# A transformer pair on one core: decays and SiLU moved in two rounds of the Delta net, U before AT, shorter head norms in the stick, gates spread

## The chip, the cores and the metric

One Trainium2 chip, one NeuronCore. The metric is the device time of one execution in microseconds; it is the median of several runs. Nothing is shared with other cores, and all inputs lie in HBM at the start.

## The reference, cut to what matters

The function is a first block (modulated SwiGLU, an attention with short convolution, SwiGLU; 512 tokens and a context of 256) followed by a second block on 528 tokens (16 meta tokens ahead). All is float32. The change touches the second block's mixer:

```
proj = hn @ w_in                                   # 1024 -> 89 column tiles of 128
q = l2norm(silu(conv(dq))); k = l2norm(silu(conv(dk))); v = silu(conv(dv))
g = cumsum(-exp(a_log) * softplus(da + dt_bias))   # decays, per chunk
# Delta net, 8 heads, state 128 x 256, chunk by chunk:
decay = exp(where(i >= j, g_i - g_j, -inf))
lower = where(i > j, (k*beta) @ k.T * decay, 0);   U = inverse of (eye + lower)
attn = q @ k.T * decay                             # AT is its transpose
u, w = U @ (v*beta), U @ (k*beta*exp(g))
v_new = u - w @ S;  o = (q*exp(g)) @ S + attn @ v_new;  S = S*exp(g_last) + k_dec.T @ v_new
o_dn = rmsnorm(o) * silu(dz)
# stick breaking attention, 8 heads:
qs = rmsnorm(sq, sbq_gain);  ks = rmsnorm(sk, sbk_gain)
z = qs @ ks.T * 128**-0.5;  w = exp(log_sigmoid(z) + sum of later log_sigmoid(-z)), strictly causal
merged = sigmoid(gate_dn) * (o_dn @ w_branch_dn) + sigmoid(gate_sb) * (o_sb @ w_branch_sb)
h = h + merged @ w_out
```

## The kernel before

**Products.** Activations lie with features on the partitions. Each weight tile of 1024 x 128 is loaded by SyncE's queue into one of three `w_raw` buffers, copied by ScalarE into `w_hi` (fp32r) and the rest is computed into `w_lo` by VectorE or GpSimd (`lows`; the table `LOW`, line 394, says which, by number of the tile). Four pairs of hi and lo exist (`PARTS`). A product is `w_hi*x_hi + w_hi*x_lo + w_lo*x_hi`, eight row tiles k of it, each one `mm` event (`quantum`, line 1098). `highs(m)` and `lows(m)` work up to four tiles ahead of tile m, and wait for the product that used the buffer before.

**One order for all engines.** The second block's mixer is driven by two lists of events, `DELTA` and `STICK`, that Python makes before the kernel is emitted. `timed` and `merged` put small events between the `mm` and `branch` events, at times in us given by tables (`PREPARE`, `SCAN`, `L2NORM`, `LATE_SCAN` and so on). Every engine walks the same list in the same order and does its own part of each event; engines are in order, so an event that waits on one engine holds what stands behind it in the list. Semaphores (`p_u`, `k_norm`, ...) count finished steps.

**A round of the Delta net.** Round i runs the scan of head i (`v0`, `s0`, `k1`, ... `s4`, `nsq`, `norm`, `gain`, `parts`, `hiz`), prepares head i+1 (`pair`, `turn`, then six levels `x1`, `u1`, ... `u6` that invert the triangle), broadcasts and exponentiates the decays of head i+2 (`bcast`, a DMA from HBM on ScalarE's queue, and `decay`), normalises its q and k (`l2q`, `lnq`, `stq`), and multiplies the branch weights of head i-1 (`branch`). `decay` is done by ScalarE (five Relu, two Exp into `DT`, one Exp of `gB`; line 1967 on), VectorE (the mask on `DT`, two steps) and GpSimd (`LT`). The last chunk has 16 tokens only, so work on chunks comes in two blocks: four chunks of 128 and one of 16 (`WIDE`).

**pair and turn.** `pair` (tensor: line 1359) makes k k' and k q' for both blocks: the first block's products in one half bank each, both products of the small block in a third. VectorE (`pairs`, line 2696) makes from them, for the first block, `LT`, U in two steps and `AT`, then the same four steps for the small block; `p_u` counts these eight steps. `turn` (line 1368) transposes U of each block, ScalarE copies it out, GpSimd masks `LT` into `LM`, then come `x1` and its copies.

**Banks.** `Banks` hands out PSUM at build time. Small events of the Delta net use a ring of four half banks in turn; each entry remembers the semaphore value at which its bank is free. `pair` takes three entries, of which the second is given back at `p_u` 8h+4 (AT of the first block) and the third at 8h+8; `s0` takes two, `turn` two. Big products and branches have a ring of two double banks: a projection tile holds one, so that successive branch products use the other and wait for VectorE's add into `acc`. A tile's bank is free once ScalarE has copied it (`projected`); the copy of a z tile of head h waits until `parts` of head h-1 has used `ZZ`.

**Stick norms.** Squares (ScalarE), a product with ones (`nq`, `nk`), Ln and Exp on ScalarE for y = v^-1/2, then VectorE: v from PSUM, one Newton step in three instructions, and the gain; for q one more for the factor 128^-0.5. `k_v` frees the bank, `k_norm` counts three per head.

**Gates.** Sixteen tiles (73 to 88) are gates; ScalarE keeps the first four raw and takes the sigmoid of the others as they come; VectorE multiplies `acc` and `accs` (`gate`), in the last two rounds of the stick and behind them.

**Start of the second block.** After the last product of the second SwiGLU, ScalarE does root_ln and root_exp, then `highs`; VectorE does `root_v` and `root`, then `lows`, then writes the normed input whose first tile PE waits for.

## Time and profile before

| | us |
|---|---|
| median of 3 runs | 2865.19 (2865.05 to 2865.75) |
| the profiled execution, its own time | 2861.57 |
| its span, first to last instruction | 2859.3 |
| TensorE busy | 2790.1 (98%) |
| VectorE busy | 1489.2 (52%) |
| ScalarE busy | 1139.2 (40%) |
| GpSimd busy | 513.2 (18%) |
| mean granted TensorE clock | 0.993 |

The profile is of one execution. Busy times are sums of instruction durations without overlap; matmuls are pipelined, so a stall of less than half a us hardly shows as idle time. The chain that ended last is PE for 87% of the span. The first block and its two SwiGLU take 0 to 1343 us, the Delta net 1343 to 2081, the stick and gates 2081 to 2443, the output product and the last SwiGLU the rest.

### The profile page before, as it was taken

Reading aid. Unit: us, or ns where it says so; the run is one execution under the profiler, and the core shown is the slowest. Engines: PE = TensorE matmul, PEld = TensorE weight load, DVE = VectorE, ACT = ScalarE, POOL = GpSimd, SP = SyncE. Lnnn points to the kernel's source line nnn. Section 1 sums busy time; section 2 is a strip of 40 time slices with the busy share of each in tenths; the row PEclk is TensorE's granted clock in tenths of the full one; section 3 lists DMA queues with packets and bytes.
Section 4 is the critical chain, followed back from the end, with each engine's and each line's share of the span. In section 5 each row is a group of like instructions: output and inputs, shape, how many; then the busy total and the mean of one; then the engine's idle time right before and its main releaser. Section 6 shows DMA issues by size and latency. Waiting matters only on the chain.

```text
span 2859.3 us, 37052 instructions
## 1 busy us (share of the span) xinstructions
PE 2790.1 (98%) x14453; PEld 2233.2 (78%) x14453; DVE 1489.2 (52%) x2096; ACT 1139.2 (40%) x1697; POOL 513.2 (18%) x297
## 2 busy tenths in 40 slices
PE   8999999999999999999999999999999999999999
PEld 4888888866656688887898888887868877788887
DVE  6734534257546633335754656554267775653443
ACT  4221212224444432223655555554466663432221
POOL 0000000023111100002444444434422223100000
PEclk9999999999999999999999999999999999999999
DMA  6422313143102322222211211111211112232222
GB/s 234 151 78 83 120 63 111 53 139 120 37 30 88 127 93 92 96 92 100 80 53 45 67 56 64 53 53 38 74 60 60 60 60 93 95 103 93 91 97 81
DMA packets 69871, 241.77 MB, mean 85 GB/s; under 512 B 8218, under 2 KB 8346, under 8 KB 69314
## 3 DMA queue, kind: packets, MB, share of 16 engines
q1 hardware_dynamic: 62032, 221.28, 22.9%
q10 hardware_dynamic: 7666, 18.13, 1.9%
q8 instruction: 116, 1.90, 0.3%
q14 instruction: 57, 0.47, 0.1%
HBM read 232.74 MB, written 6.64 MB: 84 GB/s over the span
## 4 chain that ended last, share of the span: by engine, by line
PE 87%; DVE 5%; ACT 5%; DMA 1%; issue 1%; ACTq 0%; DVEq 0%; POOL 0%; SPq 0%; POOLq 0%
PE ps L1098 61%; PE ps L1484 3%; PE ps L1288 2%; PE ps L1381 2%; PE ps L1257 2%; PE ps L1585 2%; PE ps L1421 1%; PE ps L1275 1%; PE ps L1128 1%; PE ps L1309 1%; PE ps L1413 1%; ACT r L461 1%; DVE UT L468 1%; PE ps L1266 1%; ACT w_hi L461 1%
## 5 line engine op out<-in xcount | busy, mean ns | idle before, releaser
L1098 PE MATMUL ps<-Nh,w_hi 128*128 128x512 f32 (+1 forms) x1808 | 660.5, 365 | 9.5 <-DVE Nl L468 4.9
L1098 PE MATMUL ps<-Nl,w_hi 128*128 128x512 f32 (+1 forms) x1808 | 630.0, 348 | 0.0
L1098 PE MATMUL ps<-Nh,w_lo 128*128 128x512 f32 (+1 forms) x1808 | 628.0, 347 | 0.0
L461 ACT ACTIVATE w_hi<-w_raw 128x1024 fp32r<-128x1024 f32 (+1 forms) x352 | 368.7, 1047 | 637.4 <-PE ps L1098 521.8
L468 POOL TENSOR_TENSOR w_lo<-w_raw,w_hi 128x1024 fp32r<-128x1024 f32 x125 | 308.0, 2464 | 750.4 <-ACT w_hi L461 746.7
L468 DVE TENSOR_TENSOR w_lo<-w_raw,w_hi 128x1024 fp32r<-128x1024 f32 (+1 forms) x227 | 281.8, 1242 | 257.5 <-ACT w_hi L461 247.8
L1098 PEld LDWEIGHTS ps<-Nh,w_hi 128*128 128x128 f32 x1808 | 342.6, 190 | 80.2 <-issue 30.1
L1098 PEld LDWEIGHTS ps<-Nl,w_hi 128*128 128x128 f32 x1808 | 342.7, 190 | 50.6 <-issue 5.8
L1098 PEld LDWEIGHTS ps<-Nh,w_lo 128*128 128x128 f32 x1808 | 342.4, 189 | 44.1
L1098 PE MATMUL ps<-x1h,w_hi 128*128 128x512 f32 (+1 forms) x784 | 272.3, 347 | 1.9 <-DVE x1l L479 1.9
L1098 PE MATMUL ps<-x1l,w_hi 128*128 128x512 f32 (+1 forms) x784 | 266.6, 340 | 0.0
L1098 PE MATMUL ps<-x1h,w_lo 128*128 128x512 f32 (+1 forms) x784 | 264.8, 338 | 0.0
L1098 PEld LDWEIGHTS ps<-x1h,w_hi 128*128 128x128 f32 x784 | 147.0, 187 | 37.4 <-issue 16.1
L1098 PEld LDWEIGHTS ps<-x1h,w_lo 128*128 128x128 f32 x784 | 147.5, 188 | 18.4 <-DVE w_lo L468 0.2
L1098 PEld LDWEIGHTS ps<-x1l,w_hi 128*128 128x128 f32 x784 | 147.3, 188 | 18.0 <-issue 1.4
L468 POOL TENSOR_TENSOR f_t<-f_t,f_t 128x768 f32<-128x768 f32 (+1 forms) x14 | 25.0, 1786 | 658.9 <-ACT f_t L461 658.9
L1098 PE MATMUL ps<-h1h,w_hi 128*128 128x512 f32 x352 | 118.7, 337 | 0.0
L1098 PE MATMUL ps<-h1l,w_hi 128*128 128x512 f32 x352 | 118.7, 337 | 0.0
L1098 PE MATMUL ps<-h1h,w_lo 128*128 128x512 f32 x352 | 117.7, 334 | 0.0
L468 DVE TENSOR_TENSOR f_t<-f_t,ps 128x768 f32<-128x768 f32 (+1 forms) x44 | 36.1, 821 | 134.2 <-PE ps L1098 133.3
L461 ACT ACTIVATE f_t<-ps 128x768 f32<-128x768 f32 (+1 forms) x44 | 31.1, 708 | 178.7 <-PE ps L1098 178.3
L479 DVE SCALAR_TENSOR_TENSOR ada_acc<-w_raw,sc,ada_acc 128x512 f32<-128x512 f32 x112 | 84.2, 752 | 5.6
(353 smaller groups left out, 4725.0 us busy)
## 6 DMA issues: line engine op xcount, KB each, us to landing
w_raw<-in_w_in SPq DMA_DIRECT2D x132, 512.0 KB, 3.5
w_raw<-in_w_proj SPq DMA_DIRECT2D x89, 512.0 KB, 3.4
w_raw<-in_w_ada SPq DMA_DIRECT2D x52, 512.0 KB, 4.1
w_raw<-in_w_out SPq DMA_DIRECT2D x48, 448.0 KB, 3.2
w_raw<-in_w_out SPq DMA_DIRECT2D x24, 512.0 KB, 3.4
w_raw<-in_w_mix_in SPq DMA_DIRECT2D x19, 512.0 KB, 3.5
w_raw<-in_w_bdn SPq DMA_DIRECT2D x16, 512.0 KB, 3.4
w_raw<-in_w_mix_out SPq DMA_DIRECT2D x8, 512.0 KB, 3.5
```

The costliest lines, as they stand in the source:

```text
L461: self.then_inc(self.e.activation(out, in_, func, **kw), sem)
L468: self.then_inc(self.e.tensor_tensor(out, a, b, op), sem)
L479: self.then_inc(self.e.scalar_tensor_tensor(out=out, in0=a, scalar=s, in1=b, op0=op0, op1=op1), sem)
L1098: ins = e.matmul(out[:, 512 * j:512 * j + n], a[:, kk, :], x[:, kk, c0:c0 + n], start=k == 0 and p == 0, stop=k == nt - 1 and p == 2)
L1128: ins = e.matmul(bank[0:2, 0:512], t.sc[:, 2 * k:2 * k + 2], a[:, i, :], start=k == 0, stop=k == KT - 1)
L1257: ins = e.matmul(out[:, c0:c0 + nn], t.qT[r0:r0 + 64, h // 2, qb * P:(qb + 1) * P], t.kT[r0:r0 + 64, h // 4, c0:c0 + nn], start=True, stop ...
L1266: ins = e.transpose(out[:, c0:c0 + P], t.pr[n % 2][:, i * P:(i + 1) * P], cs("ident"))
L1275: ins = e.matmul(ps[:, 6, :], t.vp[:, i, 2 * (h // 4) + h % 2, :], t.PT[h % 2][:, i, :], start=h % 2 == 0 and i == 0, stop=h % 2 == 1 and ...
L1288: ins = e.matmul(out, a[:, k, :], x[:, k, 0:TX], start=k == 0 and p == 0, stop=k == KT - 1 and p == 2)
L1381: ins = e.matmul(bank[0:n, c * n:(c + 1) * n], t.LM[lv % 2][0:n, c0 + c, 0:n], UT[0:n, 1, c0 + c, 0:n], start=True, stop=True)
L1484: ins = e.matmul(out[:, 0:TX], a[:, 2 * (k % 4) + x, :], b[:, x, MS], start=x == 0 and p == 0, stop=x == 1 and p == 2)
L1585: ins = e.matmul(out[:, 0:TX], a[:, k, :], b[:, 0, MS], start=p == 0, stop=p == 2)
```

## The change

1. Two tables more, `FIRST_ROUND` and `LAST_ROUND`, place `bcast` and `decay` in round 0 (head 2) and in round 5 (head 7). In the list, `decay` of head 2 moves from behind unit 12, `stk2` and `parts` to between `u6` and unit 12; that of head 7 from behind `parts` and the last branch to between `stk1` and `u6`. `siluv` of round 0 goes behind `s0` of round 1. In round 6 `v0` and `s0` come ahead of `turn` and `siluv` behind it.
2. `pairs` makes LT and U of both blocks, then AT of both. `p_u` counts in the new order, so the waits for the second block's U become 8h+6 and 8h+4, and the second bank of `pair` is given back at 8h+7.
3. The stick's norms: ScalarE squares y after Exp; VectorE computes (bank + 128 eps) * y^2, then (that - 384) * y, then the product with a gain that was scaled once (`gain_sb`); no separate factor for q.
4. `gate`: 73 to 75 and 76 to 78 at two points become 73-74, 75, 76-77, 78-79 and 80-81 at five.
5. Tile 3 of `w_proj` has its low part on VectorE instead of GpSimd; at the start of the second block `highs` and `lows` stand ahead of the root's steps.

```diff
...
 DECAYS = ((66, "bcast"), (73, "decay"))
+FIRST_ROUND = ((58, "bcast"), (65, "decay"))
+LAST_ROUND = ((58, "bcast"), (64.5, "decay"))
 SCAN = ((0.52, "v0"), (5.18, "s0"), (8.86, "k1"), (11.5, "v1"), (14.15, "s1"), (18.33, "k2"),
...
 L2_FIRST = ((21.01, "siluz"), (22.55, "siluqk"), (25.3, "l2q"), (25.3, "lnq"), (27.1, "stq0"), (30.4, "stq1"),
-            (30.4, "stq2"), (37, "l2k"), (40, "lnk"), (45.3, "stk0"), (45.9, "stk1"), (45.9, "stk2"),
-            (59.1, "siluv"))
+            (30.4, "stq2"), (37, "l2k"), (40, "lnk"), (45.3, "stk0"), (45.9, "stk1"), (45.9, "stk2"))
 L2_LAST = ((18.91, "siluz"), (21.38, "siluqk"), (22.99, "l2q"), (22.99, "lnq"), (25.08, "stq0"), (25.13, "stq1"),
            (27.17, "stq2"), (30.21, "l2k"), (30.71, "lnk"), (30.71, "stk0"), (33.94, "stk1"), (38.5, "stk2"))
 
 LATE_PREPARE = ((1.35, "pair"), (6.9, "turn"), (9.6, "x1"), (11.2, "u1"), (17.7, "x2"), (22.2, "u2"),
                 (28.2, "x3"), (32.7, "u3"), (35.7, "x4"), (40.2, "u4"), (46.7, "x5"), (49.7, "u5"),
                 (56.9, "x6"), (60.5, "u6"))
-LATE_SCAN = ((7.95, "v0"), (7.95, "siluv"), (7.95, "s0"), (7.95, "k1"), (9.83, "v1"), (12.1, "s1"),
+LATE_SCAN = ((0.52, "v0"), (7.3, "siluv"), (5.2, "s0"), (7.95, "k1"), (9.83, "v1"), (12.1, "s1"),
              (16.67, "k2"), (19.21, "v2"), (23.63, "s2"), (27.41, "k3"), (28.59, "v3"), (31.72, "s3"),
...
         if i + 2 < NH:
-            steps += [(at, s, i + 2) for at, s in DECAYS]
+            steps += [(at, s, i + 2) for at, s in (FIRST_ROUND if i == 0 else LAST_ROUND if i + 3 == NH else DECAYS)]
+            steps += [(5.2, "siluv", 0)] if i == 1 else []
             after += [(at, s, i) for at, s in (L2_FIRST if i == 0 else L2NORM if i + 3 < NH else L2_LAST)]
...
 _POOLED = [(split_of("w_mix_in", 4), split_of("w_mix_out", 0)),
-           (split_of("w_proj", 3), split_of("w_o2", 0))]
+           (split_of("w_proj", 4), split_of("w_o2", 0))]
 LOW = ["pool" if any(a <= m < b for a, b in _POOLED) else "dve" for m in range(len(SPLITS))]
...
 
-        self.k_raw, self.k_sq, self.k_mm, self.k_ln, self.k_v, self.k_exp, self.k_norm = (
-            new("k_raw"), new("k_sq"), new("k_mm"), new("k_ln"), new("k_v"), new("k_exp"), new("k_norm"))
+        self.k_raw, self.k_sq, self.k_mm, self.k_v, self.k_exp, self.k_norm = (
+            new("k_raw"), new("k_sq"), new("k_mm"), new("k_v"), new("k_exp"), new("k_norm"))
         self.z_mm, self.z_abs, self.z_ln, self.z_sp, self.vt_mm, self.vt = (
...
         self.eps_sq = mem.put("eps_sq", [P, 1])
+        self.gain_sb = mem.put("gain_sb", [P, 2])
         low = mem.at
...
         elif name == "pair":
-            for i, v in enumerate((1, 4, 8)):
+            for i, v in enumerate((1, 7, 8)):
                 chain.use((name, h, i), s.p_u, 8 * h + v)
...
         for i, (c0, n, C) in enumerate(WIDE):
-            w.wait_ge(s.p_u, 8 * h + 4 * i + 3)
+            w.wait_ge(s.p_u, 8 * h + 3 * i + 3)
             bank = ps[:, bank_of(("turn", h, i)), :]
...
         n = SIZES[jb]
-        w.wait_ge(s.k_norm, 3 * h + 3)
+        w.wait_ge(s.k_norm, 2 * h + 2)
         bank = ps[:, bank_of((f"z{jb}", h)), :]
...
     e.dma_start(h_spill, XV).then_inc(s.h_out, 16)
+    highs(split_of("w_proj", 0) - 1, last)
     root_ln(5, D, f[1], COLSX, None, t.eps_sq[:])
     root_exp(f[3], f[1])
-    highs(split_of("w_proj", 0) - 1, last)
     z4 = [tv[0], tv[2], f[0], f[1]]
...
     def head_norm(h, i, ev):
-        w.wait_ge(s.k_norm, 3 * h + 2 * i)
+        w.wait_ge(s.k_norm, 2 * h + i)
         for j, (c0, n) in enumerate(COLS2 if i else COLSM):
             w.wait_ge(s.k_mm, 3 * h + i + j + 1)
-            w.act(t.sr[0][:, c0:c0 + n], ps[:, B.of[(*ev, j)][0], 0:n], ACT.Ln, s.k_ln, scale=1.0 / P,
+            w.act(t.sr[0][:, c0:c0 + n], ps[:, B.of[(*ev, j)][0], 0:n], ACT.Ln, s.act_step, scale=1.0 / P,
                   bias=cs("eps", n=1))
         cc = slice(0, T2) if i else MS
-        w.act(t.sr[1][:, cc], t.sr[0][:, cc], ACT.Exp, s.k_exp, scale=-0.5)
+        w.act(t.sr[1][:, cc], t.sr[0][:, cc], ACT.Exp, s.act_step, scale=-0.5)
+        w.act(t.sr[0][:, cc], t.sr[1][:, cc], ACT.Square, s.k_exp)
 
...
     ffn(1, XV, t.h2h[:, :, 0:TX], t.h2l[:, :, 0:TX], f[0:2], f[2:4], COLSX, GX, t.GM[:, 1], last)
+    lows(split_of("w_proj", 0) - 1, last)
     root_v(5, D, f[0], COLSX, None, EPS * EPS)
     root(5, f[0], f[2], f[3])
-    lows(split_of("w_proj", 0) - 1, last)
     w.wait_ge(*summed(6, s, 6))
...
     def pairs(h):
+
+        def product(i, j, n, C):
+            bank = ps[:, B.of["pair", h, j][0], :] if i == 0 else ps[:, B.of["pair", h, 2][0], j * n:]
+            return in_chunks(bank, n, C)
+
         for i, (c0, n, C) in enumerate(WIDE):
-            b, b2 = (in_chunks(ps[:, B.of["pair", h, j][0], :] if i == 0 else ps[:, B.of["pair", h, 2][0], j * n:], n, C)
-                     for j in range(2))
-            dt, at, lt = (a[0:n, c0:c0 + C, 0:n] for a in (t.DT, t.AT[h % 2], t.LT))
+            lt = t.LT[0:n, c0:c0 + C, 0:n]
             u = t.UT[h % 2][0:n, 0, c0:c0 + C, 0:n]
             w.wait_ge(s.p_lt, 2 * h + i + 1)
             w.wait_ge(s.p_pair, 4 * h + 3 * i + 1)
-            w.tt(lt, lt, b, ALU.mult, s.p_u)
+            w.tt(lt, lt, product(i, 0, n, C), ALU.mult, s.p_u)
             w.tt(u, lt, each(cs("level", n, n, 0), n, C), ALU.mult, s.p_u)
             w.tt(u, each(cs("ident", n, n), n, C), u, ALU.subtract, s.p_u)
+        for i, (c0, n, C) in enumerate(WIDE):
+            at, dt = (a[0:n, c0:c0 + C, 0:n] for a in (t.AT[h % 2], t.DT))
             w.wait_ge(s.p_pair, 4 * h + 2 * i + 2)
-            w.tt(at, b2, dt, ALU.mult, s.p_u)
+            w.tt(at, product(i, 1, n, C), dt, ALU.mult, s.p_u)
 
...
 
+    for i, (name, factor) in enumerate((("sbq", -1.0 / 256 * float(P) ** -0.5), ("sbk", -1.0 / 256))):
+        w.ts(t.gain_sb[:, i:i + 1], sm(name), factor, None, ALU.mult, None, s.step)
+
     def head_norm(h, i, ev):
         cc = slice(0, T2) if i else MS
-        v, tt, y = t.sr[5], t.sr[0][:, cc], t.sr[1][:, cc]
+        tt, square, y = t.sr[5], t.sr[0], t.sr[1][:, cc]
+        w.wait_ge(s.k_exp, 2 * h + i + 1)
         for j, (c0, n) in enumerate(COLS2 if i else COLSM):
-            w.wait_ge(s.k_ln, 3 * h + i + j + 1)
-            w.ts(v[:, c0:c0 + n], ps[:, B.of[(*ev, j)][0], 0:n], 1.0 / P, EPS, ALU.mult, ALU.add, s.k_v)
-        w.wait_ge(s.k_exp, 2 * h + i + 1)
-        w.stt(tt, y, -0.5, v[:, cc], ALU.mult, ALU.mult, s.step)
-        w.tt(tt, tt, y, ALU.mult, s.step)
-        w.stt(y, tt, 1.5, y, ALU.add, ALU.mult, s.step)
+            w.stt(tt[:, c0:c0 + n], ps[:, B.of[(*ev, j)][0], 0:n], P * EPS, square[:, c0:c0 + n], ALU.add, ALU.mult, s.k_v)
+        w.stt(y, tt[:, cc], -384.0, y, ALU.add, ALU.mult, s.step)
         dst = t.Fs[h % 2][:, i, cc]
-        w.stt(dst, dst, sm("sbq" if i == 0 else "sbk"), y, ALU.mult, ALU.mult, s.k_norm)
-        if i == 0:
-            w.ts(dst, dst, float(P) ** -0.5, None, ALU.mult, None, s.k_norm)
+        w.stt(dst, dst, t.gain_sb[:, i:i + 1], y, ALU.mult, ALU.mult, s.k_norm)
 
...
             if gating is not None and ev[0] == "mm" and ev[3] == 1:
-                for u in {77: (73, 74, 75), 78: (76, 77, 78)}.get(gating, (gating,)):
+                for u in {77: (73, 74), 78: (75,), 79: (76, 77), 80: (78, 79), 81: (80, 81)}.get(gating, (gating,)):
                     gate(u)
...
         for i, (c0, n, C) in enumerate(WIDE[:XC[lv] - XC[lv - 1]]):
-            w.wait_ge(s.p_u, 8 * h + 4 * i + 1)
+            w.wait_ge(s.p_u, 8 * h + 3 * i + 1)
             if lv > 2:
...
```

## Rows read from the trace of the kernel before

**Rows 1.** Page, parts 1 and 5.
```profile
PE 2790.1 (98%) x14453; PEld 2233.2 (78%) x14453; DVE 1489.2 (52%) x2096; ACT 1139.2 (40%) x1697; POOL 513.2 (18%) x297
...
L468 DVE TENSOR_TENSOR w_lo<-w_raw,w_hi 128x1024 fp32r<-128x1024 f32 (+1 forms) x227 | 281.8, 1242 | 257.5 <-ACT w_hi L461 247.8
```

**Rows 2.** Waits of PE, 1343 to 2450 us: us in total, times, longest.
```profile
PE ps L1368 <- DVE UT L468: 7.6, 4, 3.5
PE ps L1368 <- DVE AT L468: 6.0, 6, 1.2
PE ps L1449 <- ACT V L461: 5.4, 3, 4.4
...
PE ps L1553 <- DVE SP L468: 4.2, 1, 4.2
PE ps L1471 <- ACT r L461: 3.1, 2, 2.1
```

**Rows 3.** Stretches: us, busy of PE, PEld, DVE, ACT, POOL, clock, DMA, GB/s.
```profile
1375.60:1379.10 3.50, 3.50 (x15) 3.20 (x14) 3.32 (x4) 3.35 (x5) 1.24 (x1) 0.51 0.09 29
1942.30:1952.50 10.20, 7.74 (x26) 6.01 (x27) 4.06 (x7) 4.32 (x8) 4.32 (x5) 0.50 0.15 53
1611.20:1618.00 6.80, 5.54 (x41) 4.89 (x39) 3.95 (x9) 2.01 (x5) 5.62 (x5) 1.00 0.47 155
```

**Rows 4.** Timeline of PE, turns of heads 1, 3: start, us, instructions, idle before.
```profile
1453.15 0.63 PE L1368 MATMUL ps<-const,UT 128*128 128x128 f32 x4 [0.99 <-DVE AT L468]
1454.04 0.17 PE L1368 MATMUL ps<-const,UT 16*16 16x16 f32 x1 [0.25 <-DVE AT L468]
...
1613.18 0.60 PE L1368 MATMUL ps<-const,UT 128*128 128x128 f32 x4
```

**Rows 5.** Timeline of VectorE, pairs of head 3.
```profile
1612.29 0.69 DVE L468 TENSOR_TENSOR AT<-ps,DT 128x512 f32<-128x512 f32 x1
...
1613.50 0.92 DVE L468 TENSOR_TENSOR UT<-LT,const 16x16 f32<-16x16 f32 x1 [0.23 <-DVE LT L468]
```

**Rows 6.** Timeline of GpSimd, same place.
```profile
1611.75 2.65 POOL L468 TENSOR_TENSOR w_lo<-w_raw,w_hi 128x1024 fp32r<-128x1024 f32 x1 [0.83 <-ACT w_hi L461]
```

**Rows 7.** Timeline of ScalarE, start of round 1.
```profile
1511.74 1.33 ACT L461 ACTIVATE r<-r 128x528 f32<-128x528 f32 x2
...
1515.44 0.60 ACT L461 ACTIVATE zz<-ps 128x512 f32<-128x512 f32 x1 [2.37 <-DVE O L468]
...
1517.31 2.06 ACT L461 ACTIVATE DT<-gB,gcol 128x128 f32<-128x128 f32 x5
...
1526.98 0.39 ACT L461 ACTIVATE V<-ps 128x256 f32<-128x256 f32 x1
```

**Rows 8.** Timeline of VectorE, start of round 1.
```profile
1512.29 1.54 DVE L479 SCALAR_TENSOR_TENSOR O<-O,small,r 128x512 f32<-128x512 f32 x2
...
1520.07 0.96 DVE L468 TENSOR_TENSOR DT<-DT,const 128x512 f32<-128x512 f32 x2 [2.41 <-ACT DT L461]
```

**Rows 9.** Timeline of ScalarE, end of round 5.
```profile
1922.81 0.64 ACT L461 ACTIVATE qk<-r 128x512 f32<-128x512 f32 x1
```

**Rows 10.** Timeline of VectorE, end of round 5.
```profile
1927.52 0.69 DVE L468 TENSOR_TENSOR acc<-acc,ps 128x512 f32<-128x512 f32 x1 [0.57 <-PE ps L1484]
...
1934.35 0.96 DVE L468 TENSOR_TENSOR DT<-DT,const 128x512 f32<-128x512 f32 x2 [1.50 <-ACT DT L461]
...
1937.97 0.69 DVE L468 TENSOR_TENSOR LT<-LT,ps 128x512 f32<-128x512 f32 x1
```

**Rows 11.** Timeline of PE, last branch product of round 5.
```profile
1928.77 0.40 PE L1484 MATMUL ps<-oh,w_hi 128*128 128x512 f32 x1
```

**Rows 12.** DMA issues: operation, count, KB each, us to landing.
```profile
r<-g_spill ACTq DMA_DIRECT2D x8, 264.0 KB, 4.1
```

**Rows 13.** Timeline of VectorE, k norm of head 1 in the stick.
```profile
2108.87 2.77 DVE L479 SCALAR_TENSOR_TENSOR sbf<-sbf,small,sr 128x528 f32<-128x528 f32 x1
```

**Rows 14.** Timeline of VectorE, start of the second block.
```profile
1337.81 0.69 DVE L475 TENSOR_SCALAR f_t<-ps 128x512 f32<-128x512 f32 x1 [2.60 <-ACT f_t L461]
```

## The prediction

> **What bounds the kernel now.** I read the busy shares first: PE is busy 98% of the span [rows 1], so a change pays only where PE stands idle or runs slow. The list of PE's waits between 1343 and 2450 us, which holds the Delta net and the stick, says where [rows 2]: 7.6 us for `UT` and 6.0 us for `AT` at the transposes of `turn`, 5.4 us for `V` at `s0`, 4.2 us for `SP` at the first `w4`, 3.1 us for `r`. Then the clock in stretches [rows 3]: after the waits for `r`, of which one is 2.1 us, TensorE runs at 0.51 (its 1.2 GHz level) for 3.5 us, and after the 3.5 us wait for `UT` at 0.50 for 10.2 us. Around a `turn` with a wait of 1.2 us it stays at 1.00. So a long stall may cost, beside its length, some 3.5 us at half speed: 1.7 us more.
>
> **The turn.** The diff computes U of both blocks, then AT of both. It looks as if the second transpose of `turn` came free one AT (0.69 us) earlier. But the banks decide. The ring of half banks has four entries and is used in turn: `pair` takes three, `s0` of the other head two, `turn` two. So the first bank of `turn` is the one that held the product for AT of block 0, and the second is the one freed by AT of block 1. The trace agrees: for head 1 the transposes start at 1453.15 and 1454.04, both released by `AT` [rows 4]. After the change AT of block 0 stands behind the three small operations of block 1, so the first four transposes wait for these too.
> For head 3 that is worked out so. Before, AT of block 0 runs 1612.29 to 1612.98 [rows 5] and PE starts its four transposes at 1613.18, without idle time after `s0` [rows 4]; it stands 1.2 us, for AT of block 1, ahead of the small one [rows 2]. The 16x16 `UT<-LT,const` begins at 1613.50 and ends at 1614.42 though it moves 16 columns; GpSimd's `w_lo` began at 1611.75 and ends at 1614.40 [rows 5, 6]. AT<-ps ran in that time in its usual 0.69. After: the small U is issued at 1612.5 and still ends at 1614.42, its second step takes 0.2, AT 0.69 to 1615.31, and 0.14 us behind it the transposes start, 1615.45: PE stands 2.3 to 2.4 us there and no longer ahead of the small one. Against 1.2 that is 1.0 to 1.2, I take 1.0, and the same pattern (the `w_lo` of GpSimd over the small U step) stands in heads 3, 4, 5 and 6: 4.0 us. Head 1 has no `w_lo` there: only order, 0.3 us. Head 0 has no `s0` in between, so its banks do not wait for AT, but its small U is held by a `w_lo` as well: 0. Sum 4.3 us; bounds: -0.7 for each of six heads (-4) if the small steps slip in ahead of `w_lo`, +1.5 for each of five (+7.5).
> The stall also becomes one piece of 2.35 us where 1.2 us stood. By rows 2 and 3 the clock fell after 2.1 us and did not after 1.2, so it may fall here. I take two falls in the four heads, 2 x 1.7 = 3.4 us; bounds 0 and 6.8.
> The Trainium skill (SBUF — State Buffer, section "Who interferes with whom") states that a VectorE instruction with two SBUF inputs and a GpSimd instruction that reads SBUF exclude each other, that the one issued first keeps the port to its end, and that an input in PSUM avoids it. The trace agrees with it in rows 5 and 6. This speaks against the change: AT, which has a PSUM input, is the step that could run under `w_lo`, and it is moved behind one that can't. Without that rule the sum here would be some 5 us lower.
>
> **Round 1, decay of head 2 and SiLU.** Before, ScalarE is the chain: `zz` at 1515.44, which waits for VectorE's `O`, then w_hi, the decay from 1517.31, `oh`, `zz`, w_hi, a table load and SiLU (2.4 us), and `V` at 1526.98 [rows 7]. After, decay begins when the norm before it ends, 1513.1. VectorE meets its own part of the decay ahead of the gains, so it sits from 1512.3 until the exponential: from the first DT to VectorE's mask are 2.76 us [rows 7, 8], thus 1515.9, and the mask takes 0.96. The four steps on `O` (3.1 us, from 1512.29 to the start of `zz` before) end at 1520.0, or 1521.3 if GpSimd's LT (1.3 us) falls on them. The `zz` copy frees the bank in which unit 19 starts; PE gets there at 1517.3 and now waits 3.4 to 4.7 us. From there w_hi, oh, zz, w_hi (1.06, 1.30, 0.60, 1.06 and gaps) bring `V` to 1525.2 or 1526.5: 0.5 to 1.8 us earlier than 1526.98. The 4.4 us stall at `s0` goes, a new one at unit 19 and one at `turn` stand in its place. I take -0.9 us; bounds -4 (VectorE not late) and +1.5 (one more slow stretch).
>
> **Round 5 to 6, decay of head 7.** The broadcast is issued when `norm` is through (its last step is sent at 1922.81 [rows 9]); it lands after 4.1 us [rows 12], 1926.9, ScalarE is idle then, and VectorE's mask comes 2.76 us later, 1929.7 to 1930.7. VectorE stands meanwhile: `u6`, the `acc` add and the gains are queued behind the decay. The `acc` add of branch 6, at 1927.52 before [rows 10], comes behind `u6` (half a us with its gaps) at 1931.3 and ends at 1932.0; branch 7 needs that bank, and PE stands from 1928.77 [rows 11] for 3.3 us, so the clock falls too. From `acc` to `LT` VectorE needs 10.45 us before; without mask (0.96) and the wait for it (1.50) 8.0. `LT` comes at 1939.3, or 1941.9 when GpSimd's work falls on it, instead of 1937.97. From there to AT of block 1 are 5.8 us as before, so `turn` can start at 1945.3 to 1947.9. PE (which has `v0` and `s0` done ahead) is there at about 1940.8: 4.5 to 7.1 us, I take 6.5. The place costs 3.3 + 6.5 + 2.8 at half speed = 12.6 us. Before it costs 3.5 (`UT`) and, in the slow stretch, 10.20 - 7.74 idle and 7.74 / 2 [rows 2, 3], 9.9. Difference +2.7; bounds -6 (the 3.5 us and the slow stretch gone) and +5.
>
> **Stick norms.** Each norm loses one tensor op and the scaling of its own (0.69 + 0.43 for q, 0.71 for k), and ScalarE gains a Square of 0.65. VectorE's first step now waits for this Square. For head 0 `nk` comes 0.65 us later, `z0` then needs not wait the 1.0 us that it does: -0.4. Of the 4.2 us for `SP`, VectorE's last k step (2.77 us, 2 of it held by `w_lo`, [rows 13]) ends some 2.3 us earlier, but the next step has two SBUF inputs and is held instead; `w4` is early by 0.2 at most beyond that. From head 2 on PE waits for none of this. I take -0.2; bounds -4 and +1.
>
> **Gates.** Two of the gates (each 0.69 us, a form as AT in rows 5) leave the place where VectorE's adds let branch products through, and go where it has less to do. Half of 1.4, -0.7; bounds -1.4 and 0.
>
> **Start of the second block.** Unit 3's w_lo goes to VectorE (1.24 us [rows 1]), and stands ahead of the root. VectorE is idle for 2.60 us until 1337.81 [rows 14], but ScalarE's w_hi comes behind its last square and, as I estimate, ends at 1337.0; so 0.5 us of the 1.24 remain on the chain that PE waits for; with less work left in the slow stretch behind it I take +0.3; bounds 0 and +2. GpSimd's missing w_lo frees nobody.
>
> **Sum.** 0.3 + 4.3 + 3.4 - 0.9 + 2.7 - 0.2 - 0.7 = +8.9 us on the profiled execution's 2861.57 us (span 2859.3), which lies 3.6 us under the median of the runs. On the median, 2865.19 + 8.9 = 2874 us.
>
> **Rivals.** (1) The waits go as the diff has it: six AT waits (6.0), the 4.4 us at `s0` with its slow stretch (some 7), half of the place at head 7 (5): about 2850 us. For it: these are the longest waits in rows 2. Against: the banks and VectorE's order. It decides if VectorE's decay comes before it has anything queued behind. (2) The parts cancel: turn +4.3, no additional falls of the clock, head 7 even, the others -1.5: 2868 us, within what counts as no change. For it: no row has a stall of 2.35 us, so a fall behind it is not sure, and one slow stretch that disappears elsewhere is worth 1.7. (3) Every turn's stall is followed by a slow stretch and head 7 is at its bound: 2865.2 + 8.9 + 3.4 + 2.3 = 2880 us.
>
> **Chances.** Forecast 0.45 (its own range 2870 to 2879), rival 1 0.13, rival 2 0.33, rival 3 0.09. A measurement of this kernel tells 0.2%, 5.7 us, from no change. Faster 0.13, same 0.33, slower 0.54. The range reaches to rival 2 and halfway to rival 1: 2858 to 2882.
>
> **What would show it.** Right: transposes of heads 3 to 6 start right behind AT of block 0, 2.3 us later than now against `s0`, with the small U ending with `w_lo`; new waits of PE for `zz` at unit 19 and for `acc` at branch 7; the wait for `V` under 1 us. Wrong: turn starts at once behind `s0`; the 16x16 U takes 0.16 us in heads 3 to 6; no wait at branch 7; slow stretches fewer than seven between 1340 and 2370 us.

## The result and the profile after

The changed kernel takes 2889.95 us (median of 4 runs, 2887.43 to 2890.83) against 2865.47 us: ratio 1.0086, 95% interval 1.0074 to 1.0098. It is slower by 24.5 us. Slower was forecast, but by 8.9 us, and the time lies outside the range. The profiled execution took 2889.43 us and has a span of 2887.4, 28.1 us longer than before. That is more than 24.5, because the profiled execution of the kernel before was 3.6 us under its median.

Four starts on PE, of the same instruction in both traces (taken from the timelines), show where the time went:

| start of | before | after | later by | new here |
|---|---|---|---|---|
| first product of the second block | 1343.35 | 1353.31 | 9.96 | 9.96 |
| product 6 of tile 12 (round 0) | 1515.89 | 1526.71 | 10.82 | 0.86 |
| `u1` of head 2 (round 1) | 1536.91 | 1553.35 | 16.44 | 5.62 |
| `x1` of head 6 | 1867.99 | 1892.42 | 24.43 | 7.99 |
| first product of tile 53 (round 6 done) | 2056.75 | 2083.63 | 26.88 | 2.45 |
| last product of the last gate | 2440.84 | 2468.79 | 27.95 | 1.07 |

Of the first row 0.94 us is the longer wait for `Nl` (5.84 for 4.90), which belongs to the start of the second block. The other 9.0 us were in no term of the sum: PE's products ahead of that wait are the same in both kernels. PE's list of waits between 1343 and 2460 us (us in total, times, longest) answers to [rows 2]:

```profile
PE ps L1371 <- DVE AT L470: 18.5, 7, 4.4
PE ps L1101 <- DVE Nl L470: 5.8, 1, 5.8
PE ps L1556 <- DVE SP L470: 4.3, 1, 4.3
PE ps L1101 <- ACT zz L463: 4.3, 1, 4.3
PE ps L1487 <- DVE acc L470: 3.1, 1, 3.1
...
PE ps L1371 <- DVE UT L470: 2.6, 2, 1.8
```

The waits for `V` of 4.4 and for `UT` of 3.5 us are gone. In their place stand `zz`, `acc` and three times as much `AT`. `Nl` is the wait at the start of the second block, 4.9 us before.

Slow stretches after the turns of heads 3, 4 and 6, and around the one of head 5, which answer to [rows 3] (us, busy of PE, PEld, DVE, ACT, POOL, clock, DMA, GB/s):

```profile
1632.21:1635.62 3.41, 3.41 (x17) 3.24 (x16) 0.10 (x1) 0.77 (x2) 1.69 (x3) 0.50 0.32 129
1717.54:1720.95 3.41, 3.18 (x14) 2.84 (x15) 0.67 (x3) 0.77 (x2) 2.27 (x4) 0.50 0.44 154
1888.21:1891.62 3.41, 3.28 (x14) 2.94 (x15) 0.58 (x2) 0.77 (x2) 2.17 (x4) 0.50 0.47 154
...
1799.00:1806.00 7.00, 4.80 (x36) 4.18 (x35) 4.89 (x8) 2.45 (x5) 5.70 (x6) 1.00 0.44 150
```

Three of the four stalls were followed by a stretch at 1.2 GHz; the prediction took two.

The turn of head 3, on PE, VectorE and GpSimd, which answers to [rows 4 to 6]:

```profile
1631.70 0.75 PE L1371 MATMUL ps<-const,UT 128*128 128x128 f32 x5 [2.15 <-DVE AT L470]
```

```profile
1627.71 0.69 DVE L470 TENSOR_TENSOR UT<-const,UT 128x512 f32<-128x512 f32 x1
1628.53 0.16 DVE L470 TENSOR_TENSOR LT<-LT,ps 16x16 f32<-16x16 f32 x1
1628.72 1.91 DVE L470 TENSOR_TENSOR UT<-LT,const 16x16 f32<-16x16 f32 x1
1630.66 0.16 DVE L470 TENSOR_TENSOR UT<-const,UT 16x16 f32<-16x16 f32 x1
1630.86 0.89 DVE L470 TENSOR_TENSOR AT<-ps,DT 128x512 f32<-128x512 f32 x2
```

```profile
1627.95 2.65 POOL L470 TENSOR_TENSOR w_lo<-w_raw,w_hi 128x1024 fp32r<-128x1024 f32 x1 [0.83 <-ACT w_hi L463]
```

In the changed kernel the 16x16 U step takes 1.91 us and ends within 0.03 us of GpSimd's `w_lo`; both AT stand behind it, and PE's transposes behind the first AT.

Round 1, PE's two stalls and VectorE, which answers to [rows 7, 8]:

```profile
1532.52 0.36 PE L1101 MATMUL ps<-Nh,w_hi 128*128 128x264 f32 x1 [4.25 <-ACT zz L463]
...
1544.59 1.21 PE L1371 MATMUL ps<-const,UT 128*128 128x128 f32 x5 [3.84 <-DVE AT L470]
```

```profile
1526.73 0.96 DVE L470 TENSOR_TENSOR DT<-DT,const 128x512 f32<-128x512 f32 x2 [3.65 <-ACT DT L463]
...
1537.23 0.69 DVE L470 TENSOR_TENSOR LT<-LT,ps 128x512 f32<-128x512 f32 x1 [3.22 <-PE ps L1362]
1537.95 1.66 DVE L470 TENSOR_TENSOR UT<-LT,const 128x512 f32<-128x512 f32 x1
1539.65 2.72 DVE L470 TENSOR_TENSOR UT<-const,UT 128x512 f32<-128x512 f32 x1
```

GpSimd runs `ol` (1536.38 to 1539.07) and `w_lo` (1539.21 to 1541.82) in that time. The same two U steps took 1.55 and 1.64 us in the kernel before.

The head 7 place on PE, which answers to [rows 11] and the `UT` of [rows 2]:

```profile
1956.60 0.80 PE L1487 MATMUL ps<-oh,w_hi 128*128 128x512 f32 x1 [3.10 <-DVE acc L470]
...
1967.04 0.71 PE L1460 MATMUL ps<-AT,V 128*128 128x128 f32 x4 [1.40 <-DVE LT L470]
1972.14 1.21 PE L1371 MATMUL ps<-const,UT 128*128 128x128 f32 x5 [4.39 <-DVE AT L470]
```

### The profile page after: what moved, and what is told of

The parts are those of the page before. It is cut to its first block, busy times and chain, and to the rows that moved or that the text cites. A ratio compares the mean times of both kernels' runs of the same rounds, so it can differ in the third digit from the quotient of the medians.

```text
span 2887.4 us, 36993 instructions
## 1 busy us (share of the span) xinstructions
PE 2809.2 (97%) x14453; PEld 2242.0 (78%) x14453; DVE 1469.7 (51%) x2059; ACT 1146.5 (40%) x1713; POOL 510.8 (18%) x296
## 4 chain that ended last, share of the span: by engine, by line
PE 89%; DVE 6%; ACT 3%; DMA 1%; issue 1%; ACTq 0%; DVEq 0%; POOL 0%; SPq 0%; POOLq 0%
PE ps L1101 63%; PE ps L1487 3%; PE ps L1291 2%; PE ps L1588 2%; PE ps L1384 2%; PE ps L1260 2%; PE ps L1131 1%; PE ps L1424 1%; PE ps L1278 1%; PE ps L1312 1%; PE ps L1416 1%; DVE UT L470 1%; DMA w_raw<-in_w_ada 1%; PE ps L1269 1%; PE ps L1445 1%
## 5 line engine op out<-in xcount | busy, mean ns | idle before, releaser
L1101 PEld LDWEIGHTS ps<-x1h,w_hi 128*128 128x128 f32 x784 | 146.9, 187 | 36.8 <-issue 16.2
```

Source lines behind the costliest of these rows:

```text
L1101: ins = e.matmul(out[:, 512 * j:512 * j + n], a[:, kk, :], x[:, kk, c0:c0 + n], start=k == 0 and p == 0, stop=k == nt - 1 and p == 2)
```

## The experiments

Ratios are to the kernel before on the same chip; its median was 2863.3 to 2865.2 us on four chips, but single runs of it lie between 2860 and 2872. The ratios, with a 95% interval in brackets, are not exactly those of the medians. Where two runs of different chips are subtracted, up to 1.9 us of the difference can come from that.

### Where the tiles lie

The 9 us ahead of 1343 us came with no stall, so I compared durations of one product. PE's groups on `h1h` and `h1l` from 180 to 250 us (us busy, mean ns of one | idle), first before, then after:

```profile
L1098 PE MATMUL ps<-h1l,w_hi 128*128 128x512 f32 x62 | 24.4, 394 | 0.0
L1098 PE MATMUL ps<-h1h,w_hi 128*128 128x512 f32 x62 | 24.3, 392 | 0.0
L1098 PE MATMUL ps<-h1h,w_lo 128*128 128x512 f32 x62 | 24.1, 388 | 0.0
```

```profile
L1101 PE MATMUL ps<-h1h,w_hi 128*128 128x512 f32 x60 | 23.9, 398 | 0.0
L1101 PE MATMUL ps<-h1h,w_lo 128*128 128x512 f32 x60 | 23.8, 396 | 0.0
L1101 PE MATMUL ps<-h1l,w_hi 128*128 128x512 f32 x60 | 23.6, 393 | 0.0
```

At the same granted clock (1.00) `w_hi*x_hi` takes 6 ns more and `w_lo*x_hi` 8 ns more, `w_hi*x_lo` 1 ns less. These durations overlap, so a second measure is the time from start to start: the six products of one row tile k (three of 512 columns, three of 256) take 1040.0 ns before and 1059.9 ns after, read from the timelines of 190 to 250 us. The diff has one thing that reaches this place: `gain_sb`, a tile of two floats, is put in front of all activation tiles and takes 32 bytes there.

```diff
 self.eps_sq = mem.put("eps_sq", [P, 1])
+mem.at += 32                              # pad32, ahead of the activations
+mem.at += 64                              # pad64
 low = mem.at
```

> The kernel before, with nothing changed but 32 empty bytes ahead of all activation tiles, as the new small tile of the changed kernel puts there (the weight tiles stay where they were). Why: in the changed kernel's trace TensorE is later by 9 us at 1343 us already, in code that the change does not touch; the mean pitch of h1h times w_hi (512 columns) between 180 and 260 us went from 229.7 to 236.6 ns, at a granted clock of 1.0 in both. Theory P (place in SBUF): the same 9 us, +0.25 to +0.45% (2872 to 2878 us), and the same pitches of 236 to 237 ns. Rival D (the drift comes from something else in the changed kernel, its instruction stream or that run): 0.0 +-0.1%, pitch 229 to 230 ns.

Measured: 2873.65 us, 1.0034 (1.0022 to 1.0046). An empty gap of 32 bytes makes a third of a per cent. The durations (398, 396, 393 ns) and the 1059.9 ns for the six are those of the changed kernel.

```diff
-self.eps_sq = mem.put("eps_sq", [P, 1])
-self.gain_sb = mem.put("gain_sb", [P, 2])
+self.eps_sq = mem.put("eps_sq", [P, 3])   # after_place: gain_sb is eps_sq[:, 1:3]
```

> The changed kernel whole, but its new tile of two floats lies in the unused bytes of the slot of eps_sq, so that every other tile lies where it did before the change. Theory P: the 9 us ahead of 1343 us go, -0.25 to -0.45% against the changed kernel, that is +0.45 to +0.65% on the kernel before, 2878 to 2884 us; what is left is the turns, round 1 and head 7. Rival D: no difference to the changed kernel, 2888 to 2891 us.

Measured: 2879.51 us, 1.0052 (1.0036 to 1.0069), 10.4 us under the changed kernel, with the durations of before:

```profile
L1100 PE MATMUL ps<-h1l,w_hi 128*128 128x512 f32 x61 | 24.0, 394 | 0.0
L1100 PE MATMUL ps<-h1h,w_hi 128*128 128x512 f32 x61 | 23.9, 392 | 0.0
L1100 PE MATMUL ps<-h1h,w_lo 128*128 128x512 f32 x60 | 23.3, 388 | 0.0
```

So 8 to 10 of the 24.5 us are the place of the tiles, shown from both sides: 10.4 on the medians (the gap alone 10.3), 8.3 when each version is held against the kernel before measured beside it.

> As the run with 32 empty bytes, with 64. Theory P1 (what counts is whether the tiles that TensorE streams begin on a multiple of 64 bytes; before they do, in the changed kernel they begin 32 past one): 0.0 +-0.1%, 2862 to 2869 us, pitch 229 to 231 ns. Rival P2 (any shift against the place of before costs, or the distance to the weight tiles does): +0.2 to +0.45%, 2871 to 2878 us.

Measured: 2869.1 us, 1.0019 (1.0009 to 1.0028). Theory P1 falls: a gap of 64 bytes costs too, about half. The time lies between the two forecast ranges; all three durations are 395 ns.

```diff
+mem.at += 32                              # all32 and all32_again; all64: 64
 self.raw = [mem.put(f"w_raw{i}", [P, 8, P]) for i in range(RAW)]
```

> The kernel before with 32 empty bytes ahead of the weight tiles (w_raw, w_hi, w_lo) and all that lies above them, so that weights and activations are shifted together and their distance is as before. Theory P1 (place of the streamed tile on a multiple of 64 bytes): about as the run with 32 bytes ahead of the activations, +0.25 to +0.45%, 2872 to 2878 us, perhaps more as the weights' loads are off the multiple too. Rival P3 (the distance between weights and activations counts): 0.0 +-0.1%, 2862 to 2869 us.

Measured: 2852.92 us, 0.9961 (0.9946 to 0.9976): neither. With weights and activations shifted together the kernel before becomes faster by 10 us:

```profile
L1099 PE MATMUL ps<-h1h,w_hi 128*128 128x512 f32 x64 | 24.8, 388 | 0.0
L1099 PE MATMUL ps<-h1h,w_lo 128*128 128x512 f32 x63 | 24.8, 394 | 0.0
...
L1099 PE MATMUL ps<-h1h,w_hi 128*128 128x256 f32 x63 | 17.4, 276 | 0.0
```

The durations at 512 columns only change places (388, 394 and 392 ns for 392, 388 and 394); those at 256 columns fall from 279 or 280 to 276. From start to start the gain is plain, see the table below.

> The kernel before with 64 empty bytes ahead of the weight tiles, so that all weights and activations lie 64 bytes further. Theory P4 (the pitch depends on the place of each tile within 64 bytes and on their distance): neutral, 0.0 +-0.1%, h1h times w_hi at 229 to 230 ns. Rival P5 (the place within a larger unit, 128 bytes or more, counts): pitch of one product between 225 and 237 ns, +-0.2 to 0.4%.

Measured: 2864.61 us, 0.9996 (0.9988 to 1.0005), with 392, 394 and 388 ns again: neutral, as P4 has it.

| run | empty bytes ahead of weights, of activations | six products of a row tile, ns | first product of the second block, us |
|---|---|---|---|
| before | 0, 0 | 1040.0 | 1343.35 |
| pad32 | 0, 32 | 1059.9 | 1352.28 |
| pad64 | 0, 64 | 1055.0 | 1346.51 |
| all32 | 32, 32 | 1026.7 | 1335.75 |
| all64 | 64, 64 | 1040.0 | 1343.78 |
| after | 0, 32 | 1059.9 | 1353.31 |
| after_place | 0, 0 | 1040.0 | 1345.73 |

The last two have 0.94 us of the longer `Nl` wait in the last column. In its first 50 us after_place has 6.8 us at half the clock, after, pad64, all32 and all64 have 3.4 us, before and pad32 none; these runs can't tie that to the gaps. A stretch of 3.4 us is worth some 1.5 us (worked out in the last section). In the Delta net the place is not seen: from `x1` of one head to `x1` of the next 83.5 to 83.6 us pass in before, pad32 and all32, where no slow stretch lies between. The runs fit a cost that depends on the place within 64 bytes and on the distance of weights and activations. Only shifts of 32 and 64 bytes were measured, so another rule is not excluded, and the cause is open.

> The kernel before with 32 empty bytes ahead of the weight tiles, again, beside the next run. Theory (independent gains): -0.35% to -0.4% on the kernel before, 2853 to 2856 us. Rival (its first run was lucky in its slow stretches, or in its chip): -0.2 to -0.3%, 2856 to 2860.

Measured: 2857.63 us, 0.9975 (0.9966 to 0.9984). The gain is there a second time, but 7.6 instead of 10.4 us, on another chip. The trace has again 1026.7 ns, and the second block's first product at 1335.46, 0.3 us from all32: 7.6 and 7.9 us ahead of the kernel before. So the gain from the place repeats; the difference between 10.4 and 7.6 us doesn't come from there.

### Undoing one part

Each is `after_place` with one part as before, so it is held against 2879.5 us. These four ran on another chip than `after_place`, whose kernel before took 2864.05 instead of 2863.32 us; when each is held against its own kernel before, every gain below is 0.7 us larger.

```diff
-for i, v in enumerate((1, 7, 8)):         # no_pairs, with the waits on p_u of before
+for i, v in enumerate((1, 4, 8)):
...
             w.tt(u, each(cs("ident", n, n), n, C), u, ALU.subtract, s.p_u)
-        for i, (c0, n, C) in enumerate(WIDE):
-            w.wait_ge(s.p_pair, 4 * h + 2 * i + 2)
+            w.wait_ge(s.p_pair, 4 * h + 2 * i + 2)
             w.tt(at, product(i, 1, n, C), dt, ALU.mult, s.p_u)
```

> The changed kernel with its new tile in the old place (the run after_place, 2879.5 us, is what it is to be held against), and pairs as before: LT, U, AT of the four chunks, then of the small one, with p_u, its waits and the given-back bank as before. Theory T (the turn is held by AT of the first block, which now stands behind the small U steps that GpSimd's w_lo holds): PE's wait for AT in heads 3 to 6 falls from 2.3 to 1.2 us each, and one to three slow stretches of 1.7 us go: -5 to -9 us, 2870 to 2874. Rival S (the stalls at turn are set by the slow U steps alone, whatever the order; what grew is work shifted by round 1): 0 to -1.5 us, 2878 to 2880.

Measured: 2871.47 us, 1.0024 (1.0014 to 1.0033): -8.0 us. Theory T holds: from `u1` of head 2 to `x1` of head 6 its trace takes 330.8 us (338.1 in after_place, 331.1 before), and no slow stretch follows a turn of heads 3 to 6, where after_place has two.

```diff
-(FIRST_ROUND if i == 0 else LAST_ROUND if i + 3 == NH else DECAYS)   # no_first
+(LAST_ROUND if i + 3 == NH else DECAYS)
-steps += [(5.2, "siluv", 0)] if i == 1 else []
```

> As after_place, but round 0 and 1 as before: bcast and decay of head 2 at 66 and 73, siluv of round 0 at 59.1. Theory R (VectorE sits before the decay of head 2, the gains come late, zz frees its bank late, and LT and AT of head 2 come late behind that, which the prediction left out): PE's 4.2 us wait for zz goes, the one of 4.4 us for AT at the turn of head 2 becomes 4.4 us for V and 1 us for UT as before: -4 to -6 us, 2873.5 to 2875.5. Rival: as predicted, round 1 is about even (+-1.5 us) and the loss lies elsewhere, 2878 to 2881.

Measured: 2876.54 us, 1.0039 (1.0027 to 1.0052): -3.0 us on the median, less than the 4 to 6 expected. In its trace the 4.4 us wait for `V` is PE's only wait in this place again, and round 1 takes what it took before within 0.1 us.

```diff
-(FIRST_ROUND if i == 0 else LAST_ROUND if i + 3 == NH else DECAYS)   # no_last, and LATE_SCAN as before
+(FIRST_ROUND if i == 0 else DECAYS)
```

> As after_place, but rounds 5 and 6 as before: decay of head 7 at 73, v0, siluv, s0 at 7.95. Theory L (predicted and seen in the trace): the 3.0 us wait for acc at branch 7 and 2.7 us of stall and slow clock go, the old 3.5 us for UT in a slow stretch come back: -2 to -4 us, 2875.5 to 2877.5. Rival (pairs' new order is what makes head 7 long, the moved decay is even): 0 to -1 us; or a gain from the moved v0 and s0 hidden in it: +1 to +4 us.

Measured: 2878.34 us, 1.0044 (1.0031 to 1.0058): -1.2 us, less than expected and within what single runs scatter. In its profiled execution the place of head 7 is 2.2 us shorter than in that of after_place, and the turns of heads 3 to 6 are 4.5 us longer, with four slow stretches instead of two.

```diff
+w.stt(y, tt[:, cc], -384.0, y, ALU.add, ALU.mult, s.step)     # only_small, on the kernel before
...
+for u in {77: (73, 74), 78: (75,), 79: (76, 77), 80: (78, 79), 81: (80, 81)}.get(gating, (gating,)):
...
+           (split_of("w_proj", 4), split_of("w_o2", 0))]
```

> The kernel before (all tiles in their old place) with the three small parts alone: the stick's head norms, the spread gates, and tile 3 with highs and lows ahead of the root at the start of the second block. Theory (terms of the trace): start +0.9 us, stick and gates between +1 and -1: +0.0 to +2 us on the kernel before. If the three big parts add up, this is also after_place less the differences of the other three runs. Rival (the shorter norms and spread gates win as the diff means them): -1.5 to -4 us.

Measured: 2865.31 us, 1.0005 (0.9995 to 1.0015): +1.3 us, with the start of the second block in it. 8.0, 3.0 and 1.2 us taken from 2879.5 give 2867.3, so the parts add up within 2 us (within 0.5 when each is held against its own kernel before: 16.2 less 8.8, 3.7 and 1.9 leaves 1.8 for 1.3). The shorter norms bring nothing that can be seen: PE's wait for `SP` is 4.3 us where it was 4.2, and the 1.0 us for `sbf` that went is made up by the 1.1 for `accs`. No run has norms and gates apart.

```profile
PE ps L1555 <- DVE SP L470: 4.3, 1, 4.3
PE ps L1587 <- DVE accs L475: 1.1, 1, 1.1
```

### Round 1 taken apart

```diff
-steps += [(at, s, i + 2) for at, s in DECAYS]
+steps += [(at, s, i + 2) for at, s in (FIRST_ROUND if i == 0 else DECAYS)]   # only_decay
...
+steps += [(5.2, "siluv", 0)] if i == 1 else []                               # only_silu
```

> The kernel before with bcast and decay of head 2 alone at 58 and 65 in round 0; siluv of round 0 stays. Theory R: VectorE's mask waits for the exponential ahead of the gains, zz of tile 12 is copied 4 us late, PE waits about 4 us for zz at unit 19, and then V (ScalarE's SiLU still ahead of it) or AT at s0 and turn: +2 to +5 us, 2866.5 to 2869.5. Rival (the prediction's -0.9): the waits trade places, -2 to +1 us, 2862 to 2865.5; then the loss in round 1 is made by both moves together.

Measured: 2869.61 us, 1.0014 (1.0005 to 1.0023): +4.5 us. Theory R holds: the moved decay alone makes the loss. PE's waits between 1500 and 1540 us, where before has only the 4.4 us for `V` (`AT` is 3.84 us in the changed kernel, where the new order of `pairs` is in it as well):

```profile
PE ps L1099 <- ACT zz L462: 4.3, 1, 4.3
PE ps L1369 <- DVE AT L469: 2.5, 1, 2.5
```

> The kernel before with one list edit: siluv of round 0 goes behind s0 of round 1. ScalarE's table load and SiLU (2.4 us) stand between decay and V in round 1; they would go behind V. Theory: V comes 2.4 us earlier, PE's wait of 4.4 us at s0 becomes about 2, then AT or UT of head 2 is next at turn (AT of the first block ends at 1526.96, 0.5 us ahead of s0's start now), so -0.5 to -2.5 us and the slow stretch stays. Rival: the wait for V goes below 1 us and the slow stretch with it, -4 to -6 us.

Measured: 2863.05 us, 0.999 (0.9981 to 1.0). The 4.4 us wait becomes two, as theory has it; the gain of 1.4 us is not clear of the measurement:

```profile
PE ps L1449 <- ACT V L461: 2.0, 1, 2.0
PE ps L1368 <- DVE AT L468: 1.8, 2, 1.0
```

> The kernel before with LATE_SCAN's first three times alone: in round 6 v0 and s0 stand ahead of turn, siluv behind it. Theory (from the prediction: turn of head 7 then takes banks that the small AT frees, and its transposes come behind s0 instead of filling the wait): before, turn waits 3.5 us for UT, then s0 is short; after, s0 fills part of that wait, U of the first block is done by then: -2 to 0 us. Rival: the 3.5 us go and with them the slow stretch of 10.2 us, -4 to -8; or the turn waits for AT of the small block behind the w_lo of GpSimd, +1 to +3.

Measured: 2864.26 us, 0.9993 (0.9984 to 1.0001), no difference. The 3.5 us for `UT` is turned into others (PE, 1930 to 1965 us):

```profile
PE ps L1368 <- DVE AT L468: 3.1, 2, 2.3
PE ps L1449 <- ACT V L461: 2.6, 1, 2.6
```

### The port of GpSimd and VectorE

```diff
-    for ev in DELTA:                      # GpSimd's walk; after_hold, before_hold
-        if ended is not None and ev[0] in ("mm", "branch"):
+    held = {i for h, at in enumerate(turns, 2) for i in range(DELTA.index(("pair", h)) - 4, at)}
+    for at, ev in enumerate(DELTA):
+        if ended is not None and ev[0] in ("mm", "branch") and at not in held:
             lows(split_of(*ended), last)
```

`held` are the places from 4 ahead of `pair` up to `turn`, heads 2 to 7.

> As after_place (2879.5 us), but GpSimd keeps back the w_lo that it would start between pair and turn of heads 2 to 7 until it has made LM of level 1 behind turn; the order of all VectorE's work stays the changed one. Theory W (the new order costs because GpSimd's w_lo holds the small U step, which now stands ahead of AT): the 16x16 U step takes 0.16 us instead of 1.9 in heads 3 to 6, AT of the first block ends 1.7 us earlier, the turn's wait falls from 2.3 to 0.6 us, the two or three slow stretches behind it go, head 2's U step of 2.7 us takes 0.7: -8 to -12 us, 2867.5 to 2871.5. Rival O (the order by itself costs, three small steps of VectorE ahead of AT, or its queue): -0 to -2 us, the 2.3 us waits stay.

Measured: 2871.89 us, 1.0025 (1.0016 to 1.0034): -7.6 us, just short of the 8 to 12 expected, with VectorE's changed order left as it is. So it is not the order by itself, but the order under GpSimd's `w_lo`. The waits of heads 3 to 6 fell from 8.7 to 5.5 us in all, though, and not to 0.6 each; the next run shows why.

> The kernel before with GpSimd's w_lo kept back from pair to behind turn in the same way. Theory W: the small U step of heads 3 to 6 takes 0.16 instead of 0.9 to 1.1 us, so the 1.2 us wait for AT ahead of the small transpose falls to 0.3, and head 2 and 7 gain about 1 us each, perhaps more in their slow stretches: -4 to -7 us, 2857 to 2860 us on a before of 2864. Rival: LM of level 2, or the product that uses the tile, comes late by the 2.65 us of the postponed w_lo: 0 to +4 us.

Measured: 2864.78 us, 1.0001 (0.9992 to 1.001): no gain. VectorE and GpSimd at head 4:

```profile
1698.70 1.27 DVE L468 TENSOR_TENSOR UT<-LT,const 128x512 f32<-128x512 f32 x1
1700.00 1.66 DVE L468 TENSOR_TENSOR UT<-const,UT 128x512 f32<-128x512 f32 x1
...
1702.78 0.16 DVE L468 TENSOR_TENSOR UT<-LT,const 16x16 f32<-16x16 f32 x1
```

```profile
1697.05 2.37 POOL L468 TENSOR_TENSOR w_lo<-w_raw,w_hi 128x1024 fp32r<-128x1024 f32 x1
1699.59 1.52 POOL L468 TENSOR_TENSOR LM<-LT,const 128x512 f32<-128x512 f32 x1 [0.17 <-POOL w_lo L468]
```

The small U step is free (0.16), but GpSimd's mask `LM`, which waits only for `LT`, moved up into the gap and holds the second large U step: 1.66 us where 0.69 is usual. One holder was replaced by another. So both `w_lo` go behind `turn`, and `LM` of level 1 waits for U:

```diff
-    held = {i for h, at in enumerate(turns, 2) for i in range(DELTA.index(("pair", h)) - 4, at)}
+    held = {i for h, at in enumerate(turns, 2) for i in range(DELTA.index(("pair", h)) - 12, at)}   # before_holds, both_best, best_silu
...
-            w.wait_ge(s.p_u, 8 * h + 4 * i + 1)
+            w.wait_ge(s.p_u, 8 * h + 4 * i + (3 if lv == 1 else 1))
```

> The kernel before; GpSimd keeps back both w_lo of the stretch (12 events ahead of pair up to turn, heads 2 to 7) until behind turn, and its mask LM of level 1 waits for U of the same block (p_u 8h+3, 8h+7) instead of LT. Theory W (any GpSimd instruction that reads SBUF holds VectorE's U steps, in the run before_hold it was LM: U<-const,U took 1.65 instead of 0.69 us): both U steps of the four chunks take 0.69, the small ones 0.16, PE's ten waits for AT at turn (5.5 us) fall under 2 us, heads 2 and 7 gain 1 to 2 us each: -6 to -10 us, 2854.5 to 2858.5. Rival (x1 waits for the later LM, or the four pieces of work that GpSimd then does in a row come late for level 2 or a product): -1 to +4 us.

Measured: 2858.68 us, 0.9973 (0.9964 to 0.9983): -6.5 us. Head 4 on VectorE and PE:

```profile
1694.37 0.69 DVE L468 TENSOR_TENSOR UT<-LT,const 128x512 f32<-128x512 f32 x1
1695.10 0.69 DVE L468 TENSOR_TENSOR UT<-const,UT 128x512 f32<-128x512 f32 x1
...
1696.91 0.26 DVE L468 TENSOR_TENSOR UT<-LT,const 16x16 f32<-16x16 f32 x1
```

```profile
1697.34 0.71 PE L1368 MATMUL ps<-const,UT 128*128 128x128 f32 x5
```

All five transposes run on without a wait. Of PE's six waits for `AT` at turns (6.0 us) one of 0.3 is left, and from `x1` of head 3 to that of head 4 82.3 us pass instead of 83.6. GpSimd's two `w_lo` (4.9 us) now run behind the turn, and PE's list has no wait for GpSimd. (The Trainium skill, SBUF — State Buffer, section "Who interferes with whom", names the pair that excludes each other by its SBUF inputs and not by the operation: this run and the one before agree with it, for `LM` as for `w_lo`.)

> As before_holds, with 32 empty bytes ahead of the weight tiles as in the run all32 (2852.9 us). If both gains are real and independent they add up: -6 to -10 on 2852.9, 2843 to 2847 us. Rival (the gain of either is the luck of where slow stretches fall): 2850 to 2856 us.

Measured: 2850.98 us, 0.9948 (0.9936 to 0.996), 4 us above the expected range, which started from all32's 2852.9 us on another chip. On this chip the two gains are 6.5 and 7.6 us, the sum 14.1, and both_best is 14.2 us under the kernel before: they add up within the measurement.

> Both gains (as in both_best, 2851.0 us) and siluv of round 0 behind s0 of round 1. Theory: the move adds what it gave alone, -1 us, 2848 to 2851 us, and all together lie 4 to 7 us under all32_again. Rival: nothing added, or the V wait is replaced by one for AT of head 2, 2851 to 2853.

Measured: 2847.78 us, 0.9946 (0.9932 to 0.9959), 9.9 us under all32_again on the same chip. This is the fastest version, 17.5 us under the kernel before and 42 under the changed one. It is 3.2 us under both_best, and PE's longest wait for `V` is 2.0 instead of 4.4 us; whether the moved SiLU makes the 3.2 can't be told at these intervals.

## Why the prediction was wrong, step by step

- **What was left out.** No term of the sum was for the place of the tiles. The diff shows `gain_sb` put ahead of `low`; the prediction has no word on it, though it shifts every activation that PE streams. 8 to 10 of the 24.5 us by `after_place` and `pad32`. With 10 the sum would have been 2884.
- **The turn**: right, in kind and size. Forecast 4.3 and 3.4 us for the slow stretches; seen 8.0 for heads 3 to 6 with three slow stretches, 7.0 in after_place with two, and 8.0 by undoing it. The banks, the held 16x16 step and the start 0.14 us behind AT came as written.
- **Round 1**: the failed step of the sum, -0.9 forecast, +5.6 in the trace (+4.5 in that of after_place) and +4.5 by `only_decay`. The waits were foreseen (`zz` 3.4 to 4.7, seen 4.25; `V` under 1 us, none left here). The step "bring `V` to 1525.2 or 1526.5: 0.5 to 1.8 us earlier" counted the gain at the old end of the chain. But the stall at unit 19 comes ahead of `pair`, so it moves PE's products for head 2, VectorE's LT, its U steps (1.66 and 2.72 us under GpSimd's `ol` and `w_lo`, 1.55 and 1.64 before) and AT. The place then ended with `AT`, not with `V`: "one at `turn`" was named and given no price, though it was 3.84 us. With 10 us for the place and this term 6.5 higher the sum would have been 2890 to 2891.
- **Head 7**: 2.7 us forecast, 2.45 seen, with 3.10 us for `acc` (3.3) and 4.39 + 1.40 at `s0` and `turn` (6.5). Undoing it gave 1.2 on the median, and the intervals tell that neither from 2.7 nor from nothing.
- **Stick, gates**: -0.9 forecast, +1.07 in the trace; +1.3 by `only_small`, of which 0.9 is the start. So no gain came, and a loss can't be told from nothing. The wait for `SP` did not shorten at all.
- **Start**: +0.3 forecast, `Nl` 5.8 for 4.9: +0.9, inside its bounds.
- **Rivals.** The third (every turn's stall followed by a slow stretch, head 7 at its bound, 2880) comes nearest in time, and three of its four falls came. None of the three held the place of the tiles or a price for round 1's `turn`, so none reached 2890.

## What to carry to other kernels

A new tile in a hand-made SBUF map is a change to every product behind it: put it where nothing moves, or measure an empty gap of its size by itself first. When two engines hold each other up, as VectorE's U steps and GpSimd do here, keeping one instruction back only helps if what follows in its queue doesn't take its place. A wait that an edit removes is worth what is left until the next one ends; when the edit makes a new stall ahead of the old, the whole chain behind that stall has to be timed again, its end included.

## What the runs showed of the hardware

- The duration of a 128x512 fp32r product depends on where its operands lie: 388 to 398 ns for one at the same clock, 1026.7 to 1059.9 ns for the six of a row tile, with shifts of 32 and 64 bytes, and in the whole kernel from -10 to +10 us.
- How much of a run TensorE spends in slow stretches differs between executions of one unchanged kernel, and so does its time. In 110 executions of the kernel before, those with a mean granted clock of 0.989 took 2870.2 to 2871.0 us, those with 0.993 took 2859.9 to 2863.8. In `before_hold` two stretches lie where the kernel before has none, though PE's work there is the same (GpSimd's is not quite):

```profile
1664.20:1671.00 6.80, 6.80 (x24) 5.70 (x24) 4.83 (x6) 0.83 (x2) 3.16 (x2) 0.50 0.47 154
1834.90:1838.30 3.40, 3.40 (x16) 3.21 (x16) 3.16 (x4) 0.51 (x1) 2.80 (x2) 0.51 0.48 154
```

In the profile of before the clock is 1.00 in both places, and PE does 38 instructions instead of 24 between 1664.20 and 1671.00. From `x1` of head 3 to that of head 4, with the stretch of 6.8 us, `before_hold` takes 86.75 us where before takes 83.62, and from head 5 to head 6, with the one of 3.4, 85.18 for 83.65: 3.1 and 1.5 us. So two such stretches more or less hide or feign an edit of 3 us, and a single execution can't judge it. What decides in which execution they fall was not tested.
